# Two transformer-like blocks on one core: expert rows scatter-added to the residual, and another opening

## The chip, the core and the metric

The kernel runs on one core of a Trainium2 chip. The metric is device time in microseconds (us), the median of several runs. One core has five engines with instruction streams of their own (TensorE for matmuls, VectorE, ScalarE, Pool, and SyncE, which here only starts DMAs) and 16 DMA engines that all queues share. Streams wait for each other by semaphores.

## The reference

The input x has 1024 tokens of 1024 floats. Two blocks follow each other.

Block 1: modulation from a vector c (`silu(c) @ ada_w`), RMS norm, a short-convolution mixer, and then an expert-choice layer with 16 experts, each of which takes 128 tokens. Block 2: the same modulation with weights of its own, an mLSTM and pooling mixer, and then 32 experts of width 512, of which each token chooses two:

```
gates = softmax(top_val) * g_gate            # two weights per token
out   = (silu(xb @ w_gate[e]) * (xb @ w_up[e])) @ w_down[e]
y     = zeros.at[slot_tok].add(out * slot_gate)
x     = x + gate_f * y
return rms_norm(x, final_g)
```

## The kernel before

Everything is float32. To keep that precision, a weight chunk of 128x1024 goes from DRAM into one of 12 slots of `ring`; ScalarE rounds it to a high part (`mH`, `wH`, `uH`, ...; line 1167 in block 2), VectorE subtracts to get the low part (`mL = ring - mH`, line 1867), and TensorE does three matmuls, high by high, low by high and high by low (lines 1994, 1995, 1997). The high and low tiles have six sets (`WSETS`). SyncE issues a chunk when VectorE has freed its slot.

**Opening.** The modulation sums `silu(c)[k] * ada_w[k]` over eight chunks: VectorE does it in `acc` and `acc2` (`ada_sum`, line 1258), with chunks in a ring of `ADA_RING` = 4 slots. The sixteenth chunk is summed by TensorE itself (line 2039). Beside it ScalarE loads 15 small row tables (line 884), then eight x tiles (line 889), and squares each (line 895); Pool takes the power -1/2 (line 638), VectorE scales the rows in place (line 1286), TensorE transposes them. When `mod` and `gain` are known (lines 1306 to 1310), ScalarE and VectorE write the modulated columns `hH` and `hL` (lines 919, 1326) and the first real matmul starts.

**Block 1's experts.** Per expert 24 chunks; Pool gathers the 128 token rows from DRAM (line 691) and scatter-adds the weighed result rows to `x1_dram` (line 702).

**Block 2's experts.** A table made by matmuls says for each slot of 128 rows (a block) the token, the weight and whether it is filled. Steps `m2_step(q, r)` run over the 32 experts in pairs: in each, TensorE does eight gate/up chunks of this expert and four down chunks of the one before, and the transposes between. Pool gathers the rows of the expert after next (`gather2`, line 815) and stores the last one's result rows plainly to `yslot_dram` (`store_y`, line 825), after ScalarE has copied them from PSUM to `ys` (`y_copy`, line 1174). Experts with over 128 tokens spill into up to 15 overflow blocks, processed one by one after the loop; with these inputs there are four. The last block's rows are weighed by VectorE and scatter-added directly (lines 1947, 1948, 869).

**End.** For each of eight token tiles, Pool gathers the two result rows of each token (`gather_rows`, line 860), ScalarE and VectorE weigh and add them and multiply by the gate row (lines 1240, 1956, 1958), VectorE adds the residual (line 1968), ScalarE squares (line 1248), Pool takes the power (line 876), VectorE scales (line 1972), SyncE stores. Because unfilled blocks of `yslot_dram` are gathered too in some cases, Pool stores zeros to 16 of them, and to 128 spare rows of `x3_dram`, in the middle of the kernel (lines 777 to 781).

Of the kernel before, what the change touches and what calls it, by code (L numbers as in the profile page):

```python
# [12 lines left out]
P = 128  # L13
# [7 lines left out]
ADA_RING = 4  # L21
# [9 lines left out]
    rt_done wait_passed ada_done split_done z_done m1_lo hy_done pool_out unused_zero m2_y final_done consts  # L31
    masks var_ready rstd_ready stored m1_tok m1_y_done zero_row rows_zero rows_in small_in
    silu_ready sq_done mod_ready tr_ready tr_hi split_hi f_part cv_done c_copied route1 e1_exp m1_used m1_hi
    m1_xT m1_xT_hi slots_ready m1_silu m1_hT m1_hT_hi if_zero gate_in if_hi v_even gate_exp branch d2_out uc_ready 
    q_mm pm_ready pv hn_tr num_out final_in dve_steps cols_tr mod_mm xn_done
    tr_lo sums_out sums2_out sums_in row_cols row_tr row_copied rows_out rows_here c_here mid_tr tr_mid v_mm pool_steps neg_out mb_in mask_done exp_done small_ready small_exp sq_out intra_out kt_mm kw_out st_mm c_ready hd_out cell_w ov_l last_y last_out row_one aff_ready halves_out affT_tr m1_xT_lo m1_hid m1_hT_lo if_lo v_odd if_mm pool_mm k_mm k_out s_mm
# [47 lines left out]
def build(nc, ctx, io, out, room):  # L84
# [11 lines left out]
    x3_dram = dram("x3_dram", [T + P, D])  # L96
    h4_dram = dram("h4_dram", [T, D])
    yslot_dram = dram("yslot_dram", [NBLK * P, D])
# [99 lines left out]
    last_tok = sb("last_tok", [P, 1], U32, moe)  # L198
    moe.close()
# [39 lines left out]
    for name in SEMS.split():  # L239
# [5 lines left out]
        [("x1_done", NT), ("x1_done_2", NT), ("x_final", NT)],  # L245
# [36 lines left out]
        [("final_in", 16), ("ov_stored", 16 * NOVF)],  # L282
# [23 lines left out]
    c_in = sems("c_in", NT)  # L306
# [29 lines left out]
    used1 += [-(-(ADAS1 - s) // ADA_RING) for s in range(ADA_RING)] + [0, 0]  # L336
# [41 lines left out]
    x3_tiles = x3_dram[0:T].rearrange("(t p) d -> p t d", p=P)  # L378
    h4_tiles = h4_dram.rearrange("(t p) d -> p t d", p=P)
    yslot_blocks = yslot_dram.rearrange("(b p) d -> p b d", p=P)  # L380
# [47 lines left out]
    AHEAD = 5  # L428


# [16 lines left out]
    def _(sp):  # L447
# [25 lines left out]
        for a in range(4):  # L473
            ada_chunk(ada1, 0, a, a % KD, a // KD, first=True)
        for a in range(4, 12):
            ada_chunk(ada1, 0, a, a % KD, a // KD)
# [130 lines left out]
    def _(pool):  # L607
# [169 lines left out]
        pool.memset(pm[1], 0.0).then_inc(S["zero_row"], 1)  # L777
        pool.wait_ge(S["zero_row"], 1)
        for b in range(E2 - 1, NBLK):
            pool.dma_start(yslot_blocks[:, b, :], pm[1]).then_inc(S["unused_zero"], 16)  # L780
        pool.dma_start(x3_dram[T:T + P], pm[1]).then_inc(S["unused_zero"], 16)
# [12 lines left out]
        pool.wait_ge(S["unused_zero"], 16 * (NOVF + 2))  # L794
# [30 lines left out]
        def store_y(q, r):  # L825
            e = 2 * q + r
            pool.wait_ge(S["m2_y"], e + 1)
            if not static(q):
                settle(pool)
            pool.dma_start(yslot_blocks[:, e, :], ys[r]).then_inc(m2_out[r], 16)  # L830

        gather2(0, 0)
        gather2(0, 1)

        def m2_step(q, r):
            s = 2 * q + r
            if not (static(q) and s + 2 > E2):
                gather2(q + 1, r)
            if not (static(q) and s < 2):
                store_y(q - 1, r)  # L840
# [3 lines left out]
        def overflow(b):  # L844
# [4 lines left out]
                                    ).then_inc(xs_in[0], 16)  # L849

        blocks = overflow_blocks(pool, overflow)
        for u in range(2):
            pool.wait_ge(m2_out[u], 16 * (E2 // 2 - u) + XS_PAST)
        pool.wait_ge(S["ov_stored"], 16 * blocks + past["ov_stored"])
        settle(pool)
        pool.wait_ge(S["m2_lo"], 12 * blocks + 12 * E2 + past["m2_lo"])
        settle(pool)
        pool.wait_ge(S["slots2"], 1 + past["slots2"])

        def gather_rows(t):  # L860
            for i, dst in enumerate((one_rows[t], two_rows[t])):
                pool.indirect_dma_start(out=dst, out_offset=None, in_=yslot_dram,
                                        in_offset=bass.IndirectOffsetOnAxis(ap=slot_u[:, i, t:t + 1], axis=0)
                                        ).then_inc(c_in[t], 16)

        for t in range(AHEAD):
            gather_rows(t)
        pool.wait_ge(S["last_y"], 1)
        pool.indirect_dma_start(out=x3_dram, in_=ys[1], in_offset=None, compute_op=ALU.add,
                                out_offset=bass.IndirectOffsetOnAxis(ap=last_tok[:, 0:1], axis=0)  # L870
                                ).then_inc(S["last_out"], 16)
        for t in range(AHEAD, NT):
            gather_rows(t)
# [6 lines left out]
    def _(act):  # L880
        act.wait_ge(S["rows_zero"], 1)
        for b in range(2):
            for name, (first, n) in row_at[b].items():
                act.dma_start(rows[first:first + n, b, :], io[name]).then_inc(
                    S["c_here" if name in ("c", "c_2") else "rows_in"], 16)
        act.wait_ge(S["cols_tr"], 1)
        act.activation(silu_c[:], ps[:, 6, 0:16], ACT.Silu).then_inc(S["silu_ready"], 1)
        for t in range(NT):
            act.dma_start(xz[:, t, :], x_tiles[:, t, :]).then_inc(x_in[t], 16)

        for t in range(NT):
            act.wait_ge(x_in[t], 16)
            if t:
                act.wait_ge(S["sq_done"], t)
            act.activation(gate_c[:], xz[:, t, :], ACT.Square,
                           accum_out=stat[:, 0, t:t + 1]).then_inc(S["sq_done"], 1)

# [23 lines left out]

        split_hi(0, 0, wH[:, 0, :])
        act.wait_ge(S["mod_ready"], 3)
# [157 lines left out]
        def weights_exp(h):  # L1081
            if h == 1:
                act.wait_ge(S["unused_zero"], 16 * (NOVF + 2))
# [90 lines left out]
        def y_copy(q, r):  # L1174
# [4 lines left out]
            act.activation(ys[r].rearrange("p (a b) -> p a b", a=2), ps[:, 4:6, :], ACT.Copy).then_inc(S["m2_y"], 1)  # L1179

        for j in range(2):
            x_hi2(0, 0, j)

# [25 lines left out]
        def overflow(b):  # L1209
            used, hi = past["m2_used"] + 12 * E2, past["m2_xT_hi"] + 2 * E2  # L1210
            for c in range(12):
                if c == 6:
                    act.wait_ge(S["m2_used"], 12 * b + used)
                    act.wait_ge(m2_out[0], 16 * (E2 // 2) + XS_PAST)
                    act.wait_ge(S["ov_stored"], 16 * b + past["ov_stored"])
                    settle(act)
                    act.activation(ys[0].rearrange("p (a b) -> p a b", a=2), ps[:, 4:6, :], ACT.Copy).then_inc(S["ov_y"], 1)
                    act.wait_ge(S["ov_y"], b + 1 + past["ov_y"])
                    settle(act)
                    act.dma_start(yslot_blocks[:, b + (E2 - 1), :], ys[0]).then_inc(S["ov_stored"], 16)  # L1220
# [17 lines left out]
        def weigh_one(t):  # L1238
            act.wait_ge(c_in[t], 32)
            act.activation(one_rows[t], one_rows[t], ACT.Copy, scale=r2[:, 8, t:t + 1]).then_inc(S["row_one"], 1)  # L1240

        for t in range(AHEAD):
            weigh_one(t)
        for t in range(NT):
            if t + AHEAD < NT:
                weigh_one(t + AHEAD)
            act.wait_ge(S["x_final"], t + 1 + past["x_final"])
            act.activation(two_rows[t], one_rows[t], ACT.Square,
# [4 lines left out]
    def _(dve):  # L1253
# [28 lines left out]
        def normed_rows1(half):  # L1282

            dve.wait_ge(S["rstd_ready"], half + 1)
            for t in range(4 * half, 4 * half + 4):
                dve.tensor_scalar(xz[:, t, :], xz[:, t, :], stat[:, 2, t:t + 1], None, ALU.mult).then_inc(S["xn_done"], 1)

        dve.wait_ge(S["silu_ready"], 1)
        for a in range(2 * KD - 1):
# [3 lines left out]
            if a == 8:  # L1293
                normed_rows1(0)
            if a == 9:
                dve.wait_ge(S["cols_tr"], 3)
                dve.tensor_copy(cols[:], ps[:, 4, 0:2 * P].rearrange("p (a b) -> p a b", a=2)
                                ).then_inc(S["cols_ready"], 1)
            if a == 12:
                variances1(1)  # L1300
            if a == 13:
                normed_rows1(1)
        split_lo(0, 0, wH[:, 0, :], wL[:, 0, :])
        dve.wait_ge(S["cols_ready"], 1 + past["cols_ready"])
# [571 lines left out]
        def hidden(e, r):  # L1876
# [7 lines left out]
        steps.mark(dve.tensor_copy(slot_w[:], table[:, 1, :]))  # L1884
# [3 lines left out]
        steps.mark(dve.scalar_tensor_tensor(out=slot_t[:, 1, :], in0=slot_t[:, 0, :], scalar=tokid[:, 0, 0:1],  # L1888
                                            in1=slot_t[:, 1, :], op0=ALU.mult, op1=ALU.add))
# [57 lines left out]
        steps.mark(dve.tensor_copy(last_tok[:], slot_t[:, 1, last_at]))  # L1947
# [3 lines left out]

        def weigh(t):
            one_row = one_rows[t]
            dve.wait_ge(c_in[t], 32)
            dve.wait_ge(S["row_one"], t + 1)
            step(dve.scalar_tensor_tensor(out=one_row, in0=two_rows[t], scalar=r2[:, 9, t:t + 1], in1=one_row,
                                          op0=ALU.mult, op1=ALU.add))
            steps.mark(dve.tensor_tensor(one_row, one_row, gate_ffn_row[:], ALU.mult))
# [6 lines left out]
        def add_residual(t):  # L1965
            dve.wait_ge(x_in[t], 48)
            steps.wait()
            dve.tensor_tensor(one_rows[t], x_rows[t], one_rows[t], ALU.add).then_inc(S["x_final"], 1)
# [555 lines left out]
```

## Time and profile before

| what | value |
|---|---|
| median of three runs | 2281.07 us (2281.05 to 2284.15) |
| profiled execution | 2274.07 us |
| its span, first to last instruction | 2272.4 us |
| TensorE busy | 2023.3 us, 89% |
| VectorE busy | 1699.5 us, 75% |
| ScalarE busy | 1247.7 us, 55% |
| Pool busy | 292.3 us, 13% |
| DMA | 637.07 MB, mean 280 GB/s |

"Busy" is the time in which an engine had an instruction under way; register and semaphore instructions are not counted. The stages in time: opening 0 to 55 us, block 1's mixer to about 500, its experts to 1077, block 2's mixer and routing to 1558, its experts to 2126, four overflow blocks to 2213, the end.

### The profile page before, as it was taken

How to read it: one execution, taken by the hardware profiler on the slowest of the kernel's cores; microseconds unless marked ns; L12 is line 12 of the kernel's file. 1: busy time of each engine (PE TensorE's matmuls, PEld its weight loads, DVE VectorE, ACT ScalarE, POOL GpSimd, SP SyncE). 2: the span in 40 equal slices, each digit the busy share in tenths (PEclk: the TensorE clock that was granted, in tenths of full speed). 3: DMA queues.
4: the chain of work that ended last, by engine and by line, in shares of the span. 5: the costliest groups of instructions: out<-in, count | busy, mean ns of one | idle time of the engine just before them, and what ended most of it. 6: DMA issues, size and time to landing. Idle time of an engine off the chain costs nothing.

```text
span 2272.4 us, 30998 instructions
## 1 busy us (share of the span) xinstructions
PE 2023.3 (89%) x9509; PEld 1675.6 (74%) x9509; DVE 1699.5 (75%) x1905; ACT 1247.7 (55%) x1464; POOL 292.3 (13%) x297
## 2 busy tenths in 40 slices
PE   3999999859999999999698988956999999999990
PEld 2888878748888887787576777845888888888770
DVE  5676665479999999998434544447999999999877
ACT  2311112108887877877524322215888888888762
POOL 1000001101100111010301450101010010101013
PEclk9999999959999999999799999977999999999995
DMA  9277854529999999998811003345999999999986
GB/s 320 67 252 228 261 201 140 213 74 356 385 381 379 389 382 386 382 379 332 284 36 56 29 28 130 112 184 201 407 411 412 412 412 412 412 412 412 380 308 259
DMA packets 240943, 637.07 MB, mean 280 GB/s; under 512 B 19796, under 2 KB 56936, under 8 KB 240876
## 3 DMA queue, kind: packets, MB, share of 16 engines
q1 hardware_dynamic: 209536, 524.35, 61.5%
q0 software_dynamic: 27104, 97.58, 12.2%
q10 hardware_dynamic: 4236, 14.27, 1.6%
q8 instruction: 39, 0.64, 0.1%
q14 instruction: 28, 0.23, 0.0%
HBM read 575.78 MB, written 60.34 MB: 280 GB/s over the span
## 4 chain that ended last, share of the span: by engine, by line
PE 64%; DVE 12%; DMA 10%; SPq 5%; issue 4%; ACT 3%; POOL 2%; ACTq 0%; DVEq 0%; POOLq 0%; PEldq 0%
PE ps L1994 19%; PE ps L1997 19%; PE ps L1995 19%; DMA ring<-in_moe_w_down 6%; SPq L529 5%; DVE mL L1483 1%; PE ps L2410 1%; DMA h_dram<-h2t 1%; DMA ring<-in_ada_w 1%; PE ps L2117 1%; DVE xz L1629 1%; PE ps L2257 1%; PE ps L2439 1%; ACT mH L995 1%; PE ps L2092 1%
## 5 line engine op out<-in xcount | busy, mean ns | idle before, releaser
L1867 DVE TENSOR_TENSOR mL<-ring,mH 128x1024 fp32r<-128x1024 f32 x384 | 454.9, 1221 | 37.4 <-ACT mH L1167 33.4
L1483 DVE TENSOR_TENSOR mL<-ring,mH 128x1024 fp32r<-128x1024 f32 x384 | 455.3, 1220 | 32.6 <-ACT mH L995 23.5
L995 ACT ACTIVATE mH<-ring 128x1024 fp32r<-128x1024 f32 x384 | 401.9, 1063 | 98.7 <-PE ps L1997 64.4
L1994 PE MATMUL ps<-mH,xsH 128*128 128x512 f32 x1088 | 436.9, 402 | 7.3 <-DVE mL L1867 4.4
L1997 PE MATMUL ps<-mH,xsL 128*128 128x512 f32 x1088 | 427.4, 393 | 0.0
L1995 PE MATMUL ps<-mL,xsH 128*128 128x512 f32 x1088 | 425.6, 391 | 0.0
L1167 ACT ACTIVATE mH<-ring 128x1024 fp32r<-128x1024 f32 x384 | 391.2, 1055 | 31.5 <-PE ps L1997 31.5
L1994 PEld LDWEIGHTS ps<-mH,xsH 128*128 128x128 f32 x1088 | 205.8, 189 | 47.9 <-issue 7.3
L1997 PEld LDWEIGHTS ps<-mH,xsL 128*128 128x128 f32 x1088 | 205.5, 189 | 44.7
L1995 PEld LDWEIGHTS ps<-mL,xsH 128*128 128x128 f32 x1088 | 206.1, 189 | 39.9
L1994 PE MATMUL ps<-mH,hidH 128*128 128x512 f32 x544 | 216.7, 398 | 13.4 <-DVE hidL L1528 6.3
L1995 PE MATMUL ps<-mL,hidH 128*128 128x512 f32 x544 | 212.7, 391 | 0.0
L1997 PE MATMUL ps<-mH,hidL 128*128 128x512 f32 x544 | 168.1, 390 | 0.0
L1994 PE MATMUL ps<-hH,wH 128*128 128x512 f32 x384 | 151.7, 395 | 3.8 <-DVE hL L1326 3.4
L1995 PE MATMUL ps<-hL,wH 128*128 128x512 f32 x384 | 150.0, 391 | 0.0
L1266 DVE SCALAR_TENSOR_TENSOR acc<-ring,silu_c,acc 128x1024 f32<-128x1024 f32 x83 | 106.6, 1284 | 34.9 <-DMA ring<-in_ada_w 29.5
L1994 PEld LDWEIGHTS ps<-mH,hidH 128*128 128x128 f32 x544 | 102.7, 189 | 38.1 <-DVE mL L1483 9.9
L1997 PE MATMUL ps<-hH,wL 128*128 128x512 f32 x384 | 122.6, 390 | 0.0
L1997 PEld LDWEIGHTS ps<-mH,hidL 128*128 128x128 f32 x544 | 102.4, 188 | 21.9
L1995 PEld LDWEIGHTS ps<-mL,hidH 128*128 128x128 f32 x544 | 102.7, 189 | 19.9
L1994 PE MATMUL ps<-woH,zsH 128*128 128x512 f32 x256 | 104.2, 407 | 10.8 <-DVE woL L1543 5.9
L1995 PE MATMUL ps<-woL,zsH 128*128 128x512 f32 x256 | 101.4, 396 | 0.0
(413 smaller groups left out, 3006.8 us busy)
## 6 DMA issues: line engine op xcount, KB each, us to landing
ring<-in_w_expert_gate SPq DMA_DIRECT2D x144, 512.0 KB, 11.0
ring<-in_w_expert_up SPq DMA_DIRECT2D x144, 512.0 KB, 11.2
ring<-in_w_expert_down SPq DMA_DIRECT2D x144, 512.0 KB, 10.6
ring<-in_moe_w_gate SPq DMA_DIRECT2D x128, 512.0 KB, 12.0
ring<-in_moe_w_up SPq DMA_DIRECT2D x128, 512.0 KB, 11.6
ring<-in_moe_w_down SPq DMA_DIRECT2D x128, 512.0 KB, 13.8
ring<-in_ada_w SPq DMA_DIRECT2D x96, 512.0 KB, 5.7
yslot_dram<-xz POOLq DMA_DIRECT2D x31, 512.0 KB, 7.0
```

The costliest lines, as they stand in the source:

```text
L529: sp.dma_start(dst, src).then_inc(ring_in[s], 16)
L995: act.activation(mH[:, m % WSETS, :], ring[:, m % RING, :], ACT.Copy).then_inc(S["m1_hi"], 1)
L1167: act.activation(mH[:, wset, :], ring[:, slot, :], ACT.Copy).then_inc(S["m2_hi"], 1)
L1266: ins = dve.scalar_tensor_tensor(out=acc[:], in0=slot, scalar=silu_c[:, silu_col + k:silu_col + k + 1], in1=acc[:], op0=ALU.mult, op1=ALU.add)
L1483: dve.tensor_tensor(mL[:, m % WSETS, :], ring[:, m % RING, :], mH[:, m % WSETS, :].bitcast(F32), ALU.subtract).then_inc(S["m1_lo"], 1)
L1629: ins = dve.scalar_tensor_tensor(out=xz[:, i, back:T], in0=tA[:, 0:T - back], scalar=col("conv_w_2", 4 * (3 - back) + i), in1=xz[:, i, bac ...
L1867: dve.tensor_tensor(mL[:, wset, :], ring[:, slot, :], mH[:, wset, :].bitcast(F32), ALU.subtract).then_inc(S["m2_lo"], 1)
L1994: pe.matmul(o, high, rh, start=start, stop=False)
L1995: pe.matmul(o, high, rl, start=False, stop=False)
L1997: last = pe.matmul(o, low, rh, start=False, stop=stop)
L2092: last = pe.transpose(ps[:, 4 + c // 4, (c % 4) * P:(c % 4 + 1) * P], h2t[:, c * P:(c + 1) * P], ident[:])
L2117: last = pe.matmul(ps[:, 6, bass.ds((s - 1) * width, width)], h2T[:, k, :], router[:, k, :], start=(k == 0), stop=(k == KD - 1))
```

## The change

- The opening ring gets six slots. ScalarE loads c and two x tiles before the other small tables and runs a SiLU of a dummy column first. The row scalings go from VectorE to ScalarE (`normed_row1`). The sixteenth chunk is summed by VectorE in two halves, and TensorE sums its columns from `acc2` alone.
- ScalarE's copy of an expert's result from PSUM is scaled by the slot's weight. Pool multiplies it by the gate row in place and scatter-adds it to `x3_dram`, after the scatter-add before it has landed. The same holds for overflow blocks.
- `yslot_dram`, its zeros, the 16 gathers at the end and the weighing of their rows are gone. Unfilled slots point beyond the last row, where the scatter-add drops them. The end loads x and goes to the squares at once.
- Pool waits for the slot tables (`rows_known`) before its first gather in block 2.

```
-ADA_RING = 4
+ADA_RING = 6
...
+        def weigh_rows(r, col):
+            pool.tensor_copy(tok_out[r][:], row_of[:, col]).then_inc(S["m2_row"], 1)
+            pool.tensor_tensor(ys[r], ys[r], gate_ffn_row[:], ALU.mult).then_inc(S["m2_row"], 1)
+
+        def scatter_rows(r, row):
+            return pool.indirect_dma_start(out=x3_dram, in_=ys[r], in_offset=None, compute_op=ALU.add,
+                                           out_offset=bass.IndirectOffsetOnAxis(ap=row[:, 0:1], axis=0),
+                                           bounds_check=T - 1, oob_is_err=False)
-        def store_y(q, r):
+        def add_y(q, r):
             e = 2 * q + r
             pool.wait_ge(S["m2_y"], e + 1)
-            pool.dma_start(yslot_blocks[:, e, :], ys[r]).then_inc(m2_out[r], 16)
+            weigh_rows(r, bass.ds(e, 1))
+            pool.wait_ge(S["m2_row"], 2 * e + 2)
+            pool.wait_ge(m2_out[1 - r], 16 * q + 16 * r + XS_PAST)
+            scatter_rows(r, tok_out[r]).then_inc(m2_out[r], 16)
+        pool.wait_ge(S["rows_known"], 2)
         gather2(0, 0)
...
-            act.activation(ys[r].rearrange("p (a b) -> p a b", a=2), ps[:, 4:6, :], ACT.Copy).then_inc(S["m2_y"], 1)
+            act.activation(ys[r].rearrange("p (a b) -> p a b", a=2), ps[:, 4:6, :], ACT.Copy,
+                           scale=slot_w[:, bass.ds(e, 1)]).then_inc(S["m2_y"], 1)
...
+        for t in range(6):
+            square(t)
+        normed_row1(0)
+        normed_row1(1)
+        square(6)
+        normed_row1(2)
+        square(7)
+        normed_row1(3)
         split_hi(0, 0, wH[:, 0, :])
+        for t in range(4, NT):
+            normed_row1(t)
...
+        for half in range(2):
+            at = slice(512 * half, 512 * half + 512)
+            dve.scalar_tensor_tensor(out=acc2[:, at], in0=last_chunk[:, at], scalar=silu_c[:, KD - 1:KD],
+                                     in1=acc2[:, at], op0=ALU.mult, op1=ALU.add
+                                     ).then_inc(S[("half_sum", "ada_done")[half]], 1)
...
-        for t in range(AHEAD):
-            gather_rows(t)
-        for t in range(AHEAD):
-            weigh(t)
         for t in range(NT):
-            add_residual(t)
+            variance(t)
             if t:
                 finish(t - 1)
```

## Rows read from the trace of the kernel before

**Rows 1.** The page, part 4: share of the chain that ended last, by engine.
```profile
PE 64%; DVE 12%; DMA 10%; SPq 5%; issue 4%; ACT 3%; POOL 2%; ACTq 0%; DVEq 0%; POOLq 0%; PEldq 0%
```

**Rows 2.** Windows, one expert of block 2: us, busy us (instructions), clock, DMA share, GB/s.
```profile
1819.40:1837.20 17.80, 17.80 (x85) 14.82 (x85) 16.54 (x18) 15.06 (x18) 1.74 (x2) 1.00 1.03 412
```

**Rows 3.** DMA issues, 1600 to 1700, then 2000 to 2100: count, KB, us to landing.
```profile
ring<-in_w_expert_down SPq DMA_DIRECT2D x24, 512.0 KB, 9.8
...
ring<-in_w_expert_down SPq DMA_DIRECT2D x22, 512.0 KB, 11.9
```

**Rows 4.** Timeline, opening: start, us, engine, line, operation, [idle before, releaser].
```profile
9.23 0.75 DVE L1263 TENSOR_SCALAR acc<-ring,silu_c 128x1024 f32<-128x1024 f32 x1 [6.85 <-ACT silu_c L887]
...
38.17 2.11 POOL L638 TENSOR_TENSOR stat<-stat,neghalf 128x4 f32<-128x4 f32 x1 [9.48 <-DVE stat L1280]
...
40.31 2.74 DVE L1286 TENSOR_SCALAR xz<-xz,stat 128x1024 f32<-128x1024 f32 x4 [0.91 <-POOL stat L638]
...
47.73 3.55 PE L2039 MATMUL ps<-silu_c,ring 128*128 128x1 f32 x16
...
52.10 0.78 ACT L919 ACTIVATE hH<-ps,mod,gain 128x512 fp32r<-128x512 f32 x1 [15.59 <-DVE gain L1310]
...
54.67 0.76 PE L1994 MATMUL ps<-hH,wH 128*128 128x512 f32 x1 [3.38 <-DVE hL L1326]
```

**Rows 5.** Windows, opening, as in rows 2.
```profile
9.00:12.00 3.00, 0.00 (x0) 0.00 (x0) 2.56 (x3) 0.19 (x2) 0.22 (x1) 1.00 0.82 98
...
24.00:27.00 3.00, 0.00 (x0) 0.00 (x0) 1.73 (x2) 1.60 (x4) 0.00 (x0) 1.00 1.02 407
```

**Rows 6.** Timeline, reload between the blocks, and the end.
```profile
1084.31 3.72 ACTq L1045 DMA_DIRECT2D xz<-x_dram  x8
...
1089.07 1.06 ACT L1050 ACTIVATE tB<-xz 128x1024 f32<-128x1024 f32 x1 [10.39 <-DMA xz<-x_dram]
...
2215.99 1.28 DVE L1948 SCALAR_TENSOR_TENSOR xz<-ps,slot_w,gate_ffn_row 128x1024 f32<-128x1024 f32 x1
...
2217.97 2.02 POOL L869 DMA_INDIRECT x_dram<-xz,last_tok  x1 [0.30 <-issue]
...
2225.82 2.77 SPq L598 DMA_DIRECT2D mH<-x_dram  x6
...
2262.17 0.55 POOL L876 TENSOR_TENSOR stat<-stat,neghalf 128x1 f32<-128x1 f32 x1 [1.46 <-DVE stat L1962]
...
2262.76 1.28 DVE L1972 SCALAR_TENSOR_TENSOR xz<-xz,stat,final_row 128x1024 f32<-128x1024 f32 x1 [0.67 <-POOL stat L876]
```

**Rows 7.** Timeline, before block 2's experts.
```profile
1548.70 0.27 DVE L1888 SCALAR_TENSOR_TENSOR slot_t<-slot_t,tokid 128x47 f32<-128x47 f32 x1
1549.04 1.07 POOL L821 DMA_INDIRECT xz<-h_dram,tok_in  x1 [31.15 <-DVE tok_in L1862]
```

**Rows 8.** Timeline, block 2's mixer: Pool and VectorE at work together, and apart.
```profile
1229.52 1.23 DVE L1543 TENSOR_TENSOR uL<-ring,uH 128x1024 fp32r<-128x1024 f32 x1 [12.68 <-ACT uH L1033]
...
1255.73 2.37 POOL L767 TENSOR_TENSOR xz<-xz,tA 128x1024 f32<-128x1024 f32 x1
...
1332.12 1.89 POOL L758 TENSOR_TENSOR tB<-tA 128x1023 f32<-128x1023 f32 x1
1332.89 2.20 DVE L1543 TENSOR_TENSOR uL<-ring,uH 128x1024 fp32r<-128x1024 f32 x1 [7.49 <-ACT uH L1033]
```

**Rows 9.** Timeline, block 2's experts, VectorE just after ScalarE's copy of a result.
```profile
2111.39 2.36 DVE L1867 TENSOR_TENSOR mL<-ring,mH 128x1024 fp32r<-128x1024 f32 x2 [0.63 <-ACT mH L1167]
```

**Rows 10.** DMA queue of Pool, 900 to 1040, then 1640 to 1900: packets, MB, share.
```profile
q0 software_dynamic: 1152, 4.19, 11.4%
...
q0 software_dynamic: 4176, 15.21, 14.5%
```

**Rows 11.** Windows, block 1's experts, as in rows 2.
```profile
920.00:940.00 20.00, 19.23 (x91) 15.61 (x90) 19.73 (x22) 16.65 (x20) 3.44 (x1) 1.00 1.04 392
```

**Rows 12.** The page, part 6: median us to landing, whole kernel.
```profile
ring<-in_moe_w_down SPq DMA_DIRECT2D x128, 512.0 KB, 13.8
```

## What I predicted

> **What bounds the kernel now.** I read the page's chain of waits first, then each engine's busy time by stage, then the timeline of the three places that the diff touches, last the DMA queues. The chain [rows 1] is 64% TensorE: most of the span is a row of matmuls, and only what makes TensorE wait counts. In block 2's expert loop [rows 2] one expert takes 17.8 us; TensorE is busy in all of it, VectorE in 16.54 and the DMA engines with a share of 1.03 at 412 GB/s. So TensorE bounds this stage, with two followers close behind: VectorE has 17.80 - 16.54 = 1.26 us free per expert, the DMA engines nearly nothing. That they have nothing shows in the landing time of a weight chunk [rows 3]: 9.8 us early in the loop and 11.9 us late in it; a queue that grows by about 0.1 us per expert (2.1 us over 400 us, 22 experts) is fed slightly faster than it drains. Outside the loops TensorE idles at the start, until 54.67 us [rows 4], and at the end, from the last matmul to the last row.
>
> The profiled execution took 2274.07 us (span 2272.4), the median of the runs is 2281.07, 7.0 more. I sum differences against the profiled one and add them to the median.
>
> **The opening.** What holds it: VectorE takes its first chunk at 9.23 us [rows 4], late because ScalarE issues 15 small loads and loads a table before SiLU; by then the four-deep ring is full, and the DMA engines move 98 GB/s in 9 to 12 us, against 407 later [rows 5]. With six chunks and two x tiles issued first, about 1.1 MB more has landed by 12 us: 1.1 / 0.407 = 2.7 us earlier. 16 chunks, eight x tiles and one weight slice of 0.52 MB are 13.1 MB, 32 us at 407 GB/s; from 3 us on that is 35 to 36, and the last sum ends near 38 to 39. VectorE's row scalings (2.74 us at 40.31) and the first eight of the sixteen column matmuls (3.55 us for eight) go from the path; a split sum of 1.3 us, of which half lies beside TensorE, comes on it. But the four scalings of the second half now stand on ScalarE, about 1.1 us each (a ScalarE pass of this size is 1.06 [rows 6]), behind Pool's power, which took 2.11 us at 38.17. I place that power at 36.5 to 38.5 and the scalings end at 43; the first hH is then written at 43 instead of 52.10, and the first matmul follows 2.57 us later as now: 45.5 instead of 54.67. I take -9 us. Ends: -12 if the power runs before VectorE's sum, -5 if only the DMA's 2.7 us and VectorE's 2.74 us of scalings go. What comes next is a row of matmuls and keeps the shift.
>
> **The middle.** 17 stores of zeros (8.9 MB) leave Pool and the DMA queues. They lie beside matmuls with nobody on the path waiting for them: 0, ends -1 and +1. Before the expert loop, Pool's first gather (issued at 1549.04 [rows 7]) waits for four more small VectorE operations, of which the one at 1548.70 is the last: its issue moves from 0.9 us behind the token copy to 0.9 behind that row, +1 us (0 to 2); this gather has the chain waiting.
>
> **The expert loop.** ScalarE's copy from PSUM gets a scale by partition: same form, same 1.0 us, ScalarE has over 2 us free: 0. Pool gets, per expert, a copy of one column and an in-place product of 128x1024, and its plain store becomes a scatter-add.
>
> The product: the nearest row is Pool's 128x1024 product at 1255.73, 2.37 us [rows 8]. What it does to others: at 1332.12 Pool ran 1.89 us, and VectorE's uL (two inputs in SBUF, 128x1024, the form of the loop's mL) took 2.20 instead of its 1.23. It ended 1.08 behind Pool's end, so it stood until 0.15 before that. VectorE does 12 mL operations per expert, back to back where Pool's product falls: the one gap there is 0.63 us [rows 9]. So VectorE needs 16.54 + 2.37 - 0.15 + 0.1 (the column copy) = 18.86 us per expert, 1.06 above 17.8. Ends: 0.4 per expert if one of its four 0.69 us operations that read PSUM always lies beside the product, 1.3 if all gaps stay.
>
> [...]
>
> The scatter-add: Pool's queue takes 11.4% of 140 us for four gathers and four scatter-adds in block 1, and 14.5% of 260 us for some 15 gathers and 15 stores in block 2 [rows 10]. That is 2.0 and 1.26 us of all 16 engines per transfer, so a scatter-add is 2 x 2.0 - 1.26 = 2.7 us, 1.45 more than a store. The loop's packet time is 1.03 x 17.8 = 18.3, and becomes 19.8 us. How much share the engines can do is shown by block 1: 1.04 to 1.05 [rows 11], and there TensorE is busy in 19.2 of 20 us, so it waits. 19.8 / 1.045 = 18.9; at the loop's own 1.03, 19.2. So the DMA engines ask for 18.9 to 19.2 us per expert, VectorE for 18.9. Ends for the DMA term: 0 if the add overlaps other packets fully, 1.45.
>
> [...]
>
> The two needs lie beside each other, the larger counts, with a little for their meeting: 19.0, +1.2 us per expert. It is not lost from the first: the 12-deep ring and six-deep weight tiles hold about 4.5 us (landing may grow from 10 to about 14, as for block 1's down chunks [rows 12]). 30 experts in the loop: 30 x 1.2 - 4.5 = +31.5 us. Ends: 30 x 0.4 - 4.5 = +7.5 and 30 x 1.5 - 4 = +41; at no cost, 0.
>
> The four overflow blocks: Pool's product covers VectorE's idle time of 1.1 us and about 0.9 more in each, and in the first ScalarE waits for the scatter-add before it (now 4 us later than a store would land): 3 x 0.9 + 1.5 = +4 (0 to 9).
>
> **The tail.** The 16 gathers, their weighing and the residual add go. The last scatter-add, issued at 2217.97, could not go before VectorE's last rows, which end at 2217.27 [rows 6]: -0.3. It takes 7.8 us to the x loads at 2225.82; I take 6.8 with the queue empty. Between the blocks the first square came 4.8 us after the same loads (1084.31 to 1089.07): first square 2229.3. From there one tile costs VectorE's 1.28 us product and Pool's power, 0.55 alone, which lock each other out: 1.85 per tile. First product ends near 2233, the last at 2233 + 7 x 1.85 = 2246 instead of 2264.04: -18 us. Ends -14 (2.4 per tile) and -22 (ScalarE's pace of 1.28).
>
> **Sum.** -9 + 0 + 1 + 31.5 + 4 - 18 = +9.5: 2283.6 on the profile's scale, 2290.5 us as median.
>
> **Rivals.** (1) The loop keeps 17.8 us: Pool's product falls beside PSUM operations and the DMA engines have room. For it: TensorE never waited; VectorE has 1.26 free. Against: the landing times and the stretched uL [rows 3, 8]. -9 + 1 - 18 + 2 = -24: 2257, faster. Decides from: fewer than 0.5 us lost per expert. (2) Only part is lost, 0.4 to 0.8 per expert: -26 + 0.6 x 30 - 4.5 + 3 = -9.5: 2271. (3) The two needs add up, since a chunk that VectorE frees late is also asked for late: 30 x 2.3 - 4.5 = 64.5: 2323. For it: both use the same ring. Against: then the DMA share falls below its limit and frees itself. (4) The opening doesn't gain, since the same bytes must land: -2 instead of -9: 2297.5.
>
> **Numbers.** Chances: forecast (2280 to 2300) 0.54, (1) 0.14, (2) 0.16, (3) 0.05, (4) 0.11. 0.2% (4.6 us) is about what a measurement tells from no change. Faster than 2276.5: (1), three quarters of (2) and little of the forecast, 0.27. Within: 0.20. Slower: 0.53. Range 2262 to 2306; the forecast's own is 2280 to 2300.
>
> **What would show it.** In the loop: a period of 19.0 instead of 17.8 us, TensorE idle before matmuls for mL or for hidL, VectorE near 100% busy with single mL records of 3 us where Pool's product runs, landing of chunks at 13 us or more, ScalarE waiting for ring chunks. Opening: first matmul at 45 or 46, first VectorE sum at 7. Tail: some 18 us less from the last scatter-add to the end, a tile each 1.85 us. A loop that stays at 17.8 would prove me wrong, and so would mL records that stay at 1.22 beside Pool's product.

## The result: faster, against the forecast

The changed kernel takes 2265.09 us (median of 4, 2263.21 to 2267.04), the kernel before 2281.45 beside it: ratio 0.9927, interval 0.9915 to 0.9940, 16.4 us less. A second comparison gave 2266.71 against 2281.01, ratio 0.9938 (0.9925 to 0.9952). I had forecast 2290.5, slower, with 0.27 for faster. The range (2262 to 2306) held the time; the direction was wrong. The nearest of my cases is rival 2, part of the loop's cost, though for another reason than I gave.

The profiled execution took 2263.21 us (span 2261.5), 10.9 less than the profiled one before. By stage, from marks that both traces have:

| stretch | marks | forecast | measured |
|---|---|---|---|
| opening | start to first main matmul | -9 | -6.9 |
| middle | to first matmul of block 2's experts | +1 | +2.3 |
| expert loop | to the last expert's SiLU | +31.5 | +13.8 |
| overflow | to VectorE's last rows | +4 | +4.4 |
| tail | to the end | -18 | -24.5 |
| sum | | +9.5 | -10.9 |

The marks of the two traces: 54.67 [rows 4] and 47.81; 1558.78 and 1554.23; 2120.71 and 2129.91; 2215.99 [rows 6] and 2229.55. The middle is a coarse term: ten profiles of kernels alike up to the experts (the changed one twice, and eight made from it) have their first expert matmul at 1552.9 to 1558.7. The length of the loop repeats within 2 us.

The opening after the change, timeline (start, us, engine, line, operation, [idle before, releaser]), to be laid beside [rows 4]:

```profile
6.82 0.82 DVE L1280 TENSOR_SCALAR acc<-ring,silu_c 128x1024 f32<-128x1024 f32 x1 [4.43 <-ACT silu_c L899]
...
36.12 2.67 DVE L1283 SCALAR_TENSOR_TENSOR acc<-ring,silu_c,acc 128x1024 f32<-128x1024 f32 x2 [2.10 <-DMA ring<-in_ada_w]
...
38.95 2.11 POOL L632 TENSOR_TENSOR stat<-stat,neghalf 128x4 f32<-128x4 f32 x1 [13.13 <-DVE stat L1297]
...
40.29 1.41 DVE L1311 SCALAR_TENSOR_TENSOR acc<-ring,silu_c,acc 128x512 f32<-128x512 f32 x2
41.09 4.26 ACT L914 ACTIVATE xz<-xz,stat 128x1024 f32<-128x1024 f32 x4 [5.21 <-POOL stat L632]
...
44.76 0.17 DVE L1323 TENSOR_TENSOR gain<-gain,cols 128x8 f32<-128x8 f32 x1
45.27 0.76 ACT L937 ACTIVATE hH<-ps,mod,gain 128x512 fp32r<-128x512 f32 x1
...
47.81 0.76 PE L1988 MATMUL ps<-hH,wH 128*128 128x512 f32 x1 [3.57 <-DVE hL L1339]
```

VectorE starts 2.4 us earlier, waits for a chunk until 36.12, and only then makes the variances: Pool's power starts at 38.95, so the four scalings end at 45.3 where I had 43. The other path into the first hH is no earlier by much: the last sum ends at 41.70, where I had 38 to 39, and with TensorE's column sums behind it `gain` is ready at 44.93.

Two experts of the changed loop, windows (us, then busy us of PE, PE loads, VectorE, ScalarE, Pool; clock, DMA share, GB/s), one of a slow stretch and one of a quick one, to be laid beside [rows 2]:

```profile
1959.50:1978.47 18.97, 17.99 (x86) 14.70 (x85) 18.12 (x18) 15.20 (x18) 6.24 (x5) 1.00 1.03 370
2056.32:2074.10 17.78, 17.78 (x86) 14.82 (x85) 17.78 (x18) 15.53 (x19) 7.34 (x3) 1.00 1.00 387
```

The loop has two paces, and not one of 19.0: 17.8 us, with TensorE busy throughout, and about 19.0. What ScalarE and TensorE wait for in the slow stretch (waits, 1903 to 2042: us in total, times, longest) begins with weight chunks (those of the gate are 7.8 us more):

```profile
ACT mH L1193 <- DMA ring<-in_w_expert_up: 17.6, 21, 2.3
PEld ps L2399 <- DVE hidL L1917: 9.9, 8, 1.4
```

The tail (timeline), for the second half of [rows 6]:

```profile
2229.55 1.28 DVE L1960 SCALAR_TENSOR_TENSOR xz<-ps,slot_w,gate_ffn_row 128x1024 f32<-128x1024 f32 x1
2231.62 1.56 POOL L818 DMA_INDIRECT x_dram<-xz,last_tok  x1 [16.28 <-DVE xz L1960]
2237.22 2.85 SPq L592 DMA_DIRECT2D mH<-x_dram  x6
...
2240.53 1.06 ACT L1265 ACTIVATE ring<-mH 128x1024 f32<-128x1024 f32 x1 [19.57 <-DMA mH<-x_dram]
...
2243.07 1.28 DVE L1971 SCALAR_TENSOR_TENSOR ring<-mH,stat,final_row 128x1024 f32<-128x1024 f32 x1
...
2253.76 1.28 DVE L1971 SCALAR_TENSOR_TENSOR xz<-mL,stat,final_row 128x1024 f32<-128x1024 f32 x1 [0.44 <-POOL stat L873]
```

From the scatter-add to the x loads 5.6 us (I took 6.8), from these to the first square 3.3 (I took 4.8), and seven steps between products in 10.7 us, 1.53 each (I took 1.85).

### The profile page after: what moved, and what is told of

Its sections match the earlier page's. It is cut to its first block, busy times and chain, and to the rows that moved or that the text cites. A ratio compares the mean times of both kernels' runs of the same rounds, so it can differ in the third digit from the quotient of the medians.

```text
span 2261.5 us, 31114 instructions
## 1 busy us (share of the span) xinstructions
PE 2024.3 (90%) x9493; PEld 1669.3 (74%) x9493; DVE 1713.4 (76%) x1875; ACT 1251.7 (55%) x1465; POOL 472.7 (21%) x337
## 4 chain that ended last, share of the span: by engine, by line
PE 45%; DMA 20%; DVE 16%; issue 8%; SPq 5%; ACT 4%; POOL 1%; DVEq 0%; ACTq 0%; POOLq 0%
PE ps L1988 13%; PE ps L1989 13%; PE ps L1991 13%; DMA ring<-in_w_expert_up 6%; DMA ring<-in_moe_w_down 6%; SPq L523 5%; DMA ring<-in_w_expert_gate 4%; DVE mL L1880 3%; DVE mL L1496 1%; DMA h_dram<-h2t 1%; DMA ring<-in_ada_w 1%; ACT mH L1193 1%; PE ps L2106 1%; DVE mL L1936 1%; PE ps L2246 1%
## 5 line engine op out<-in xcount | busy, mean ns | idle before, releaser
L1880 DVE TENSOR_TENSOR mL<-ring,mH 128x1024 fp32r<-128x1024 f32 x384 | 499.4, 1340 | 15.9 <-ACT mH L1193 15.0
L1496 DVE TENSOR_TENSOR mL<-ring,mH 128x1024 fp32r<-128x1024 f32 x384 | 455.2, 1220 | 32.7 <-ACT mH L1023 23.9
L685 POOL DMA_INDIRECT xz<-h_dram,tok_in x16 | 39.5, 2468 | 377.8 <-DVE tok_in L1506 377.8
```

The costliest lines, as they stand in the source:

```text
L685: pool.indirect_dma_start(out=xs[r], out_offset=None, in_=h2_dram, in_offset=bass.IndirectOffsetOnAxis(ap=tok_in[r][:, 0:1], axis=0)).then ...
L1496: dve.tensor_tensor(mL[:, m % WSETS, :], ring[:, m % RING, :], mH[:, m % WSETS, :].bitcast(F32), ALU.subtract).then_inc(S["m1_lo"], 1)
L1880: dve.tensor_tensor(mL[:, wset, :], ring[:, slot, :], mH[:, wset, :].bitcast(F32), ALU.subtract).then_inc(S["m2_lo"], 1)
```

## Which cost is it: the product or the add?

Both suspects of my prediction sit in the loop, so each was taken away alone, then both. "Loop" is the time from the first expert matmul to the last expert's SiLU: 561.9 us before, 575.7 after; "overflow part" is from there to VectorE's last rows, 95.3 us before, 99.6 after.

**no_product.**

```
-            pool.tensor_tensor(ys[r], ys[r], gate_ffn_row[:], ALU.mult)
+            pool.tensor_tensor(ys[r][:, 0:1], ys[r][:, 0:1], gate_ffn_row[:, 0:1], ALU.mult)
```

> Leaves out the gate product on all columns but the first in Pool's handling of block 2's y rows (so the output lacks most of the gate factor); the scatter-add, its column copy and every wait stay. Lock theory (the changed kernel's loop, from the first down to the last expert, is 13.8 us longer than before because Pool's 2.40 us product stretches VectorE's mL): the loop comes back to within 2 us of the 562 us between the first loop matmul and the last SiLU of the kernel before, overflow 3 us shorter, 2247 us profiled against 2263. DMA theory (the scatter-add's extra packet time sets the pace): the loop keeps its 575.7 us, ScalarE still waits some 40 us for w_expert_up_2, time within 4 us of 2263.

2259.67 us; loop 576.9, overflow part 95.6. The product costs the loop nothing: it costs the four overflow blocks 4 us.

**plain_scatter.**

```
-            return pool.indirect_dma_start(out=x3_dram, in_=ys[r], in_offset=None, compute_op=ALU.add,
+            return pool.indirect_dma_start(out=x3_dram, in_=ys[r], in_offset=None,
```

> Leaves out the addition: block 2's y rows are written over the residual rows by the same indirect DMA without the add; the product and every wait stay. DMA theory: the loop returns to 562 to 565 us, the queue's packet time for one transfer falls from about 2.7 to about 1.3 us, time about 2250. Lock theory: the loop keeps 574 to 576 us and mL its mean of 1340 ns, time within 4 us of 2263. The last wait before the tail's x loads (5.6 us from issue in the changed kernel) becomes 1 to 2 us shorter under either.

2249.29 us; loop 561.8, overflow part 100.2. The whole loss of the loop is the add.

**neither** (both edits).

> Leaves out both: the product on all but one column and the addition. Both theories: the loop at 561 to 563 us as in the kernel before (PE busy in all of it), time about 2246. If the two costs add up, then the two runs with one of them each lose parts whose sum is 13.8 us; if the larger one alone counts, one of them loses all of it and the other nothing. A rest over 3 us here would be a third cause (the column copy, Pool's waits, or the shape of the store).

2244.33 us; loop 561.7, overflow part 95.6. In the loop there are no two parts to add up: the add alone gives the whole loss. The windows 1560 to 2110 of the changed kernel, no_product, plain_scatter and neither say why:

```profile
1560.00:2110.00 550.00, 537.98 (x2526) 443.07 (x2525) 530.93 (x510) 454.57 (x512) 227.34 (x117) 1.00 1.02 385
```
```profile
1560.00:2110.00 550.00, 536.86 (x2520) 442.25 (x2520) 493.38 (x509) 453.83 (x511) 111.80 (x117) 1.00 1.02 385
```
```profile
1560.00:2110.00 550.00, 548.62 (x2592) 455.88 (x2591) 545.48 (x522) 466.49 (x525) 276.87 (x118) 1.00 1.01 394
```
```profile
1560.00:2110.00 550.00, 548.64 (x2584) 456.23 (x2584) 508.63 (x525) 465.89 (x525) 89.88 (x117) 1.00 1.01 397
```

TensorE's column (the second number) goes with the add alone. VectorE's (the fourth) goes with the product: 545.5 - 508.6 = 36.9 us over 30.9 experts, 1.19 us each, where I had 2.3. That takes VectorE from 16.46 to 17.65 us per expert, just under TensorE's 17.8.

Why 1.19 and not 2.3, the timeline of the changed kernel shows:

```profile
2116.20 8.02 DVE L1880 TENSOR_TENSOR mL<-ring,mH 128x1024 fp32r<-128x1024 f32 x7
2119.77 4.50 POOL L814 COPY tok_out<-row_of 128x1 uint32<-128x1 uint32 x1 [8.34 <-ACT xz L1205]
2124.15 0.68 DVE L1917 TENSOR_TENSOR hidL<-ps,hidH 128x512 fp32r<-128x512 f32 x1
2124.23 2.41 POOL L815 TENSOR_TENSOR xz<-xz,gate_ffn_row 128x1024 f32<-128x1024 f32 x1
2124.75 2.98 DVE L1880 TENSOR_TENSOR mL<-ring,mH 128x1024 fp32r<-128x1024 f32 x1
```

Pool's one-column copy stands 4.5 us behind VectorE's row of seven mL. It gets in when hidL runs, which reads PSUM; the product starts beside hidL, and only one mL is stretched, from 1.22 to 2.98. The instruction that I had booked at 0.1 us works as a gate in the trace: it holds the product back until VectorE has a cheap moment. The order in time is seen, that the copy is the cause of it is my reading. The stretched mL ends 1.1 us after Pool, as in [rows 8].

**product_twice**, on plain_scatter: a second product behind the first.

```
             pool.tensor_tensor(ys[r], ys[r], gate_ffn_row[:], ALU.mult).then_inc(S["m2_row"], 1)
+            pool.wait_ge(S["m2_row"], n)
...
+            pool.tensor_tensor(ys[r], ys[r], gate_ffn_row[:], ALU.mult).then_inc(S["m2_row"], 1)
```

> The row write without the add, and Pool's 128x1024 gate product made twice for each block (so the output has the gate factor squared and lacks the addition). With one product this loop kept 17.8 us per expert with VectorE busy in 17.65 of it, 1.2 more than with a one-column product. My theory (a product waits for a VectorE operation that reads PSUM, begins beside it and costs VectorE only the rest, about 1.2 us): VectorE then needs 16.46 + 2 x 1.2 = 18.9 us, loop 562 + 31 x 1.1 = 596 us. If each product after the first begins at once and costs its whole length: 20.0 us per expert, loop 630. [...]

2308.04 us; loop 608.3, experts of 19.4 to 19.5 us from the fourth on, VectorE busy in 545.7 of 550 us. The window 1560 to 2110:

```profile
1560.00:2110.00 550.00, 522.15 (x2388) 414.08 (x2387) 545.68 (x482) 431.13 (x484) 390.39 (x137) 1.00 0.97 364
```

The product does cost VectorE: the second one adds 19.4 - 17.65 = 1.8 us to its need, more than the first with 1.19. The first starts 0.1 us into hidL (at 1962.55 in the timeline), the second 0.18 us after the first has ended, in the middle of the mL row (at 1965.12, 2.1 us into an mL); that it costs more for this reason is my reading. The result lies between my two numbers (596 and 630). So VectorE's need was hidden, with 0.15 us to spare.

## What the add costs, and what it costs it by

**extra_store**, on plain_scatter: one plain store more per expert of the loop, from the same rows.

```
             scatter_rows(r, tok_out[r]).then_inc(m2_out[r], 16)
+            pool.dma_start(spare_blocks[:, bass.ds(e, 1), :].rearrange("p a d -> p (a d)"), ys[r]
+                           ).then_inc(spare_out[r], 16)
```

> The row write without the add, one product, and one plain store more of the same 0.52 MB from Pool's queue to a scratch tensor for each expert of the loop (the output lacks the addition). Now as many bytes cross the DMA engines as with the add's read counted: 15 x 0.524 = 7.86 MB per expert. Bytes theory (the DMA engines give about 431 GB/s when that read is counted, 7.86 MB in 18.24 us): the loop is as long as with the scatter-add, 574 to 578 us. Theory of the add (its read-modify-write is what costs, the bytes fit): the loop stays at 562 to 565 us. By packet times (store 1.26 us of 16 engines more, 1.02 x 17.8 + 1.26 = 19.4, over a share of 1.03): 18.8 us per expert, loop 593.

2272.08 us; loop 582.8: between the 574 to 578 of the bytes and the 593 of the packet times, and clear of the 562 to 565 of the third theory. My premise was wrong: I had counted 128 rows for every scatter. So the 431 GB/s, an estimate from 7.86 MB and the changed loop's mean of 18.24 us per expert (17.78 + 13.8 / 30), counted rows that are not sent. The packet records of the traces show what moves. A 4 KB packet of weights takes 159 ns (median of the 46,025 in SyncE's queue in 1560 to 2110 of the changed kernel), one of a scatter-add 327 ns. And the scatter-adds do not carry 128 of them: empty slots are skipped. Rows moved per scatter-add (128 less the skipped ones, counted by their packets) and the expert period in which it was issued, from one SiLU to the next, all 29 of the changed kernel in that window:

```
issued at  rows  period us   issued at  rows  period us   issued at  rows  period us
  1597.2   128     17.78      1779.5     49     17.78      1959.5    124     19.01
  1614.9   124     17.77      1795.9      3     18.53      1978.4    108     18.91
  1633.1   111     17.78      1815.5     13     17.78      1997.3    116     18.97
  1650.6    71     17.77      1833.3     37     17.77      2016.3    128     18.95
  1668.5    49     17.78      1851.2     34     17.78      2035.2      7     18.91
  1685.2   128     18.43      1867.9     31     18.64      2054.6      2     18.32
  1702.5    77     18.45      1887.5    116     17.78      2074.2      4     17.77
  1721.3   115     18.75      1903.0     54     18.51      2092.1      8     17.77
  1740.2    20     18.94      1921.6    128     18.53      2109.7      0     17.78
  1760.1     7     18.30      1940.5     47     18.89
```

The 29 carry 63 rows in the mean, 13 of them 71 or more (the expectations say 66, from all long packets of the window, some of which are slow ones of the gathers). The packets of an add start 3.5 to 6 us after its issue, so most of its cost falls into the next period. The first five experts live on what is ahead in the ring; then the loop runs at 18.4 to 19.0 us in the two stretches of heavy experts and falls back to 17.8 one or two experts behind them. Two single slow periods, 18.53 and 18.64, do not fit that: they follow adds of 49 and 34 rows among light ones.

In packet time, as an estimate: 12 weight chunks and a gather are 13 x 128 x 0.159 / 16 = 16.5 us of each of the 16 engines, a row of the add 0.327 / 16 = 0.0204 us. 17.8 us is reached at 62 rows, and 128 rows need 19.2. In the mean the add asks for hardly more than the store that it replaced: 63 rows at 327 ns are 20.6 us of packets, 128 rows at 159 ns were 20.4. Pool's queue, gathers included, has 14.6% of the engines' time in that window after the change and 14.3% before, 2.7 and 2.5 us per expert. So a higher mean explains little of the loss.

**full_rows**: the empty slots' rows are sent too, to 128 spare rows.

```
-    x3_dram = dram("x3_dram", [T, D])
+    x3_dram = dram("x3_dram", [T + P, D])
...
-                                           bounds_check=T - 1, oob_is_err=False)
+                                           bounds_check=T + P - 1, oob_is_err=False)
...
+        step(dve.scalar_tensor_tensor(out=slot_t[:, 1, :], in0=slot_t[:, 0, :], scalar=tokid[:, 0, 0:1],
+                                      in1=slot_t[:, 1, :], op0=ALU.mult, op1=ALU.add))
```

> The changed kernel, but the empty slots' rows are added too, onto 128 spare rows behind the residual, instead of being skipped: each scatter-add moves 128 rows instead of 66 in the mean. [...] Theory of the sum: 62 rows more x 0.338 / 16 = 1.3 us per expert, so 19.5 us per expert, loop 615 us. By my prediction's term (2.7 us of packets per expert, 19.0 us per expert): 594 to 600.

2281.61 us, no faster than the kernel before (ratio 1.0001, 0.9991 to 1.0010); loop 591.4. One expert of it (windows):

```profile
1839.00:1858.00 19.00, 18.01 (x86) 14.70 (x85) 17.64 (x18) 15.19 (x19) 6.34 (x4) 1.00 1.03 386
```

Every expert from 1712 on takes 18.9 to 19.0 us, and the loop loses 29.5 us against the kernel before. That is my forecast of the loop (19.0, +31.5) nearly to the number, for a kernel that fills its blocks. The two other numbers that I had for it missed: 576 to 582 if the fullest engine counts, 615 for the sum without any slack. The first number rested on an estimate of mine of which engine serves which rows, and the counts under the next run speak against it, so the imbalance itself is not refuted.

**spread_slots.** I took the most rows in flight at once (8 for 49 rows, 17 or 18 for 128) for rows / 8, and estimated from it that each DMA engine serves eight partitions in a row. With slots filled from the first partition on, that would load the first engines more, and the spread rows would bring the loop back to 562 to 565 us. The base here is **dve_weighs_all** (below).

```
-        pool.iota(iota_s[:], [[1, P]], base=0, channel_multiplier=0,
+        pool.iota(iota_s[:], [[1, 16], [16, 8]], base=0, channel_multiplier=0,
```

> dve_weighs_all with one line more: the table that maps slots to ranks is permuted, so that the tokens of an expert no longer fill the first partitions of its block, but every eighth of the partitions evenly (rank r sits in partition 8 (r mod 16) + r / 16). [...] Theory that the adds' sum over all engines counts: loop stays at 577. If rows went to the engines in turn (row modulo 16), this order would make it worse: over 577.

2255.05 us (before beside it 2281.01); loop 574.8 against 576.8. A miss: spreading may give 2 us, hardly more than two loops of one kernel differ. But the run did not spread the rows as meant. In the changed kernel the packets of an add in flight at once are at most 2 or 3 for 7 rows, 4 for 13, 5 for 20, 8 for every add of 31 to 54 rows, 10 for 71, 12 for 77 and 16 to 18 from 108 on. That is not rows / 8. The packet records name no engine; my estimate from these counts is that one engine serves four rows in a row, that the same eight engines serve rows 33 to 64 again, and the other eight the rest. In spread_slots the adds of 13 to 54 rows have 8 in flight (one of them 9), as this order gives for my permutation too: up to 64 rows it reaches the same number of engines, eight.

So what sets the pace below 128 rows stays open. The sum over all engines alone does not give the loss: by the packet times above, each of the two stretches of eight heavy adds (1597 to 1721 with 803 rows, 1887 to 2016 with 821) asks for some 6.5 to 6.8 us more than 8 x 17.78, and full_rows shows that the ring absorbs about 6.5 (30 x 1.2 - 29.5); the sum would lose about 1 us, not 13.8. An untested rival is the fullest engine: by the order that I estimate above an add of 37 rows loads some engine with as many adds as one of 128 (8 x 0.327 us above the 16.5, so 19.2), 18 of the 29 adds do, and the 47 rows at 1940.5 stand in the middle of 19.0 us experts. It would also explain why full_rows is no slower per expert than the slow stretch here. An order that spreads 64 rows over all 16 engines would decide it.

## Two better versions

**dve_weighs_all** takes the product off Pool, and the copy off ScalarE; **dve_weighs_overflow** does it in the overflow blocks alone.

```
+        def weigh(r, at):
+            return dve.scalar_tensor_tensor(out=ys[r].rearrange("p (a b) -> p a b", a=2), in0=ps[:, 4:6, :],
+                                            scalar=slot_w[:, at],
+                                            in1=gate_ffn_row[:].rearrange("p (a b) -> p a b", a=2),
+                                            op0=ALU.mult, op1=ALU.mult)
```

> The changed kernel, but block 2's y rows are weighed by slot weight and gate row at once on VectorE out of PSUM (1.28 us), with no copy on ScalarE and no product on Pool; scatter-add and column copy stay. If the add's DMA sets the pace alone: loop 575 to 577 us as in the changed kernel, the four overflow blocks 3 to 4.5 us shorter, 2259 profiled. If VectorE's need (16.46 + 1.28 = 17.74) meets it: up to 3 us more in the loop. By the lock theory of my prediction the loop would be back at 563.

2257.67 us against 2275.18 (ratio 0.9924, 0.9911 to 0.9938); loop 576.8, overflow part 92.7. That is what the add alone would give.

> The changed kernel with that VectorE operation in the four overflow blocks alone; the loop has Pool's product as before. From the last SiLU of the loop to the last expert's rows: 95.3 to 96.5 us instead of 99.6, so 3 to 4 us shorter in all, 2259 to 2260. If VectorE's extra 1.28 us per block stands on the path as much as Pool's product does (0.7 to 1.1 us per block): no gain.

2262.51 us (ratio 0.9945, 0.9931 to 0.9958, to the same 2275.18); loop 577.5, overflow part 96.1. On this chip the kernel before is 6 us quicker than on the others, so these two ratios stand beside each other, but not beside 0.9927.

**spread_and_skip**, on spread_slots: the gather skips empty slots too, as the scatter does; for that the empty slots' entries of `tokc` point beyond the last row.

```
                                     in_offset=bass.IndirectOffsetOnAxis(ap=tok_in[r][:, 0:1], axis=0),
+                                    bounds_check=T - 1, oob_is_err=False
```

> spread_slots with the gather skipping the empty slots as well (their x rows keep what was there; these rows' results are not written). It takes 62 packets x 0.16 / 16 = 0.6 us per expert more from the DMA engines. If spread_slots is bound by TensorE again: the same loop within 1 us, the first gather up to 0.5 us later, same time. If DMA still holds it: up to 0.6 us per expert shorter, down to 562.

2244.12 us against 2281.01: ratio 0.9835 (0.9820 to 0.9850), the best of all, 22.6 us under the changed kernel on the same chip. Loop 561.5, so the add is still there and costs nothing, since the skipped gather rows pay for it: against spread_slots (574.8) that is the only change. TensorE is busy in 548.63 of the 550 us from 1560 to 2110, as much as in the run neither.

## The other parts, alone

**changed_again.**

> The changed kernel as it is, beside the runs above, for a ratio on the same chip: 0.993 against before in the first comparison; the loop from first matmul to last SiLU 575 to 578 us (575.7 in its first profile, 576.8 to 577.5 in other kernels with the same add).

2266.71 us (ratio above); loop 576.6.

**opening_alone**: the kernel before with the opening's edits (four of them are in the diff ahead: ADA_RING, the order of ScalarE's loads, the row scalings, the split sum).

> The kernel before with only the opening part of the change (six-deep ring, two x tiles and SiLU table first, row scalings on ScalarE, split last sum). First main matmul at 47.8 us as in the changed kernel instead of 54.67, and the whole 5 to 7 us shorter: 2267 to 2269 profiled. If the opening's bytes had only been shifted onto the next stage, the gain would be under 3 us at the end. It also tells how much of the 2.3 us that the changed kernel gives back between 54 and 1554 us belongs to the opening: the first loop matmul at 1552 if none, at 1554 if all.

2274.78 us against 2280.89, ratio 0.9971 (0.9958 to 0.9983): -6.1. First main matmul at 48.83, first expert matmul at 1554.86: the opening's gain reaches the experts but for 2 us, and so does that of the changed kernel. Its profile shows one thing that the one of the kernel before does not: VectorE stands 13.70 us behind the overflow blocks instead of 7.42, waiting for nothing that the profile names (timeline):

```profile
2218.58 0.15 DVE L1974 CAST last_tok<-slot_t 128x1 uint32 x1 [13.70 <-issue]
```

The medians of the kernel before lie about 7 us above its profiled 2274.07 on three chips (2281.4, 2280.9, 2281.0) and 1 above it on one (2275.2); those of the kernels with the new tail (idle time there 5.6 to 7.6 in each profile) lie within 5 us of theirs. A stall of 6.3 us in the old tail in most runs would explain why the timed gain is 14 to 16 us and the profiled one 10.9. It was seen in one profile only; I leave it open.

## Why the prediction was wrong, step by step

- **The scatter-add, 2.7 us of all engines per expert: the step that failed.** I read it from block 1 [rows 10, 11], where every slot of every expert is filled. Block 2's slots hold what routing sends, 63 of 128 rows in the mean, and the rest is skipped. At 128 rows the step is right: full_rows has 19.0 us per expert and +29.5 in the loop. At the 63 that are sent, the add costs the DMA engines in the mean hardly more than the plain store did, not 1.45 us more, and only part of the experts are slow: +13.8. Why those are, by the sum or by the fullest engine, is open (above). The diff showed it (rows beyond T - 1 are skipped) and the code before too, which gave empty slots rows behind T; I never asked how many those are. The mis-sizing is 31.5 - 13.8 = 17.7 of the 20.4 us between forecast and profile; with 13.8 in its place my sum is -8.2, faster.
- **The share that I took for full**, 1.04 to 1.05, came from a stretch where VectorE was busy in 19.73 of 20 us [rows 11], so it showed no limit of the DMA engines. full_rows has 1.03 at 19.0 us, and it hardly mattered.
- **VectorE's 18.86 us.** Wrong: 17.65. My lower end (0.4 per expert, if a PSUM operation lies beside the product) was nearer, and the copy ahead of the product, by my reading, makes it the rule while the chunks are there. It made no difference to the sum, since I took the larger of two needs, but it stood as a second support for 19.0 that did not exist.
- **The slack of 4.5 us.** A little small: full_rows loses 29.5 of 30 x 1.2 = 36, so the slack is about 6.5.
- **The product's whole length as VectorE's loss.** I had booked 2.37 of it less 0.15. The cost per product is real, 1.2 us measured for one (plain_scatter against neither) and 1.8 for a second (product_twice), but it changes with what runs when the product starts; a sum of whole durations overstates it.
- **Opening** -6.9 for -9: the power came at 38.95, beyond my 36.5 to 38.5, and the last sum ended at 41.70 for my 38 to 39; both paths reach the first hH within 0.4 us of each other, so the late chunks cost it either way. **Middle** +2.3 for +1: Pool's first gather goes 1.66 us behind the token copies instead of 0.84, so the wait costs 0.8; the rest is within what these profiles differ by. **Overflow** +4.4 for +4, its cause shown by no_product. **Tail** -24.5 for -18: each of three terms was taken a little long, and the last store ends 1.9 us sooner after its product. The 1.85 per tile took product and power as one after the other. Before, the power takes 0.55 us where VectorE is idle and 1.46 to 1.61 in the seven tiles where the residual add runs beside it; after, it takes 0.54 to 0.57 in four tiles and 1.52 in four, three times two of them together in 2.04 us, and a tile comes to 1.53.
- **The rivals.** Number 2 had the size of the loop's loss right (0.6 x 30 - 4.5 = 13.5), which is luck: none had its reason, that most of the rows are not sent and the cost differs between experts.

## What to carry to other kernels

Before an indirect DMA is priced, ask how many of its rows are real: the price per packet carried over from one stage to another (327 ns for an added row in block 1's experts before and in block 2's after), the price per transfer did not (128 x 0.327 / 16 = 2.6 us of all engines in block 1, 63 x 0.327 / 16 = 1.3 in block 2), and a mean over experts can stay the same while some of them exceed the budget. Where two engines run close behind the bound, take each new cost away alone, then double it: taking one away may show nothing, while doubling tells how close it was. And in a loop bound by DMA, look at what the neighbouring transfers carry for nothing; here skipping empty rows in the gather paid for the whole add.

## What I had not expected of the hardware

- A Pool instruction on one column (0.18 us in most experts of neither) took 4.5 us while VectorE ran seven SBUF operations back to back, and 4.8 us in the mean in plain_scatter; in the changed kernel's loop, where VectorE often waits for chunks, the mean is 2.2.
- The DMA share says little about room: it is 1.01 in neither, where TensorE is busy in 548.6 of 550 us, and 1.02 in the changed kernel, where it is in 538.0. The packet times tell more: 159 ns for 4 KB written to SBUF, 327 ns with the add.
- A skipped row still has a packet, of 8 bytes and 9 ns (1745 of them in the changed kernel from 1560 to 2110).
